# Modulation of a two-layer diffusion step: row sums on VectorE in place of matmuls, and inputs and outputs laid out ahead

## The chip, the cores and the metric

The kernel runs on one core of a Trainium2 chip. The metric is the time of one execution on the device in microseconds (us), the median of several runs.

## The reference

One inference step of a small trunk with two layers. 128 context tokens and 256 latent tokens, 384 in all, have 1024 features each, in float32. Each layer is a SwiGLU feed-forward block (hidden width 2816), a mixer (attention in layer 0, a gated spatial unit in layer 1), and a second feed-forward block. Ahead of each of these six blocks the activations are normalised and modulated, and after it a gate scales what is added:

```python
def modulation(cond, w, b):
    m = jax.nn.silu(cond) @ w + b                 # w is 1024 x 9216 for each layer
    return m.reshape(cond.shape[0], 1, N_MOD, D_MODEL)

def adaln_input(h, mod, j, g):
    return rms_norm(h, g) * (1 + mod[:, :, 3 * j + 1]) + mod[:, :, 3 * j]

hp = hp + 0.5 * adaln_gate(m_ctx, 0) * swiglu(adaln_input(hp, m_ctx, 0, norm_g[i, 0]), ffn1_w_gu[i], ffn1_w_down[i])
hs = hs + 0.5 * adaln_gate(m_lat, 0) * swiglu(adaln_input(hs, m_lat, 0, norm_g[i, 0]), ffn1_w_gu[i], ffn1_w_down[i])
```

So `modulation` is a product of two vectors (the conditions of context and of latent tokens) with two matrices of 1024 x 9216: 75 MB of weights, each used for two columns only. The rest is large matrix products with the 384 tokens.

## The kernel before

**Weights in panels.** All projections run through 169 panels of 1 MB, 256 columns (or 256 rows) of a weight matrix each. SyncE's queue loads a panel into `raw` (two buffers), ScalarE rounds it to `w_hi`, VectorE makes the remainder `w_lo = raw - w_hi` (`split`), and TensorE multiplies three times, hi by hi, hi by lo and lo by hi. Both parts have two buffers. A feed-forward block has 11 pairs of gate and up panels (`loop_pairs`, one `pair` each, called g = 0 to 10 here) and 11 down panels (`down`). The first pair of a block starts while its input x is still made, one piece of 128 features k after the other (`project_first` on TensorE, `make_x` on ScalarE and VectorE).

**Order.** Each engine runs its own instruction list in order and waits on semaphores at places written by hand. SyncE's queue issues nearly all transfers: panels p, p+1, and behind them a block of modulation weights (`mod_block`). The issue of panel p waits until VectorE has split panel p-2.

**Modulation.** The columns of the modulation matrices are cut into 72 blocks of 256. Blocks 0 to 7 (shift and scale of the first block) are needed at once. TensorE multiplies seven of them by the conditions as rows (`mod_rows`, L1037), ScalarE copies the rows to SBUF, and TensorE transposes them (L1045). The 64 blocks 8 to 71 are done beside the other work, in 30 pairs, in 8 down panels of each of three blocks, in 2 panels of the attention output, and in 4 panels each of the attention input (`MOD_STEPS`) and of the gated unit. For each, VectorE accumulates over k = 0 to 7 and both conditions into `macc` (`mod_sum`, 2 instructions at L751 and 14 at L754, of 256 elements), TensorE sums over partitions with a column of ones (`mod_psum`, 4 matmuls, shown as 8 instructions at L1055), and VectorE adds the bias (`mod_out`, L762). `mraw` holds two blocks, so the load of block b waits for the sums of block b-2:

```python
if b0 >= MOD_FIRST + 2:
    sp.wait_ge(macc_done, b0 + ii - MOD_SUM - 1)
```

**Beginning and end.** x and the small vectors arrive with tokens (or rows) on partitions and are transposed by TensorE (L1203, L1211). After the first pair's loads SyncE's queue issues small tables, and behind panels 2 and 3 the 32 loads of the attention bias (`load_bias`, L391), which GpSimd then masks (L495). At the end TensorE transposes each piece of h (L1390), ScalarE copies it to `y_tok` (L714), and eight transfers store it (L463, L464).

## Time and profile before

| | us |
|---|---|
| median of 3 runs | 1719.64 (1719.63 to 1720.17) |
| span of the profiled execution, first to last instruction | 1717.1 |
| TensorE busy with matmuls in it | 1660.1 |
| VectorE busy | 1067.5 |
| ScalarE busy | 578.3 |

The profile gives the profiled execution by its span; the median of the runs lies 2.5 us above it, for what comes before the first and after the last instruction. Busy times count an engine's own instructions; matmuls are pipelined, so TensorE's busy time is no measure of its peak.

### The profile page before, as it was taken

The page shows a single profiled execution, that of the slowest core. Times are in us where ns is not written, and L with a number is a line of the kernel's source. Part 1 is how long each engine was busy: PE and PEld are TensorE (multiplying, and loading weights), DVE is VectorE, ACT ScalarE, POOL GpSimd, SP SyncE. Part 2 cuts the span into 40 slices and gives each one's busy share as a digit, 9 for nine tenths or more (in the row PEclk, how much of TensorE's full clock was granted, in tenths as well). Part 3 has the DMA queues.
Part 4 walks back from the last instruction along what each step waited for, and adds up shares of the span by engine and source line. Part 5 has one row for each costly group of instructions (what it writes and reads, how often), then busy time and mean ns, then how long its engine had stood idle before and what let it go on. Part 6 is the DMA issues. An engine that isn't in the chain of part 4 may idle for free.

```text
span 1717.1 us, 25878 instructions
## 1 busy us (share of the span) xinstructions
PE 1660.1 (97%) x9927; PEld 1589.1 (93%) x9927; DVE 1067.5 (62%) x1803; ACT 578.3 (34%) x751; POOL 81.3 (5%) x48
## 2 busy tenths in 40 slices
PE   8899999988899899999989999998999998999998
PEld 4899999988756899999989999998999998999998
DVE  3677668767754766767966777697745435334323
ACT  2423232253344442322234333222642325333222
POOL 1200000034100100000010000001000001000000
PEclk9999999989999899999989999999999998999999
DMA  9755547526200445555634545564533332433332
GB/s 310 187 182 164 192 159 244 170 85 207 77 1 31 157 146 173 177 189 196 224 120 135 193 161 195 190 226 157 186 124 96 125 123 85 136 122 122 124 130 77
DMA packets 222917, 261.81 MB, mean 152 GB/s; under 512 B 14502, under 2 KB 207494, under 8 KB 222854
## 3 DMA queue, kind: packets, MB, share of 16 engines
q1 hardware_dynamic: 222854, 260.95, 46.3%
q8 instruction: 42, 0.69, 0.2%
q14 instruction: 21, 0.17, 0.0%
HBM read 258.64 MB, written 2.29 MB: 152 GB/s over the span
## 4 chain that ended last, share of the span: by engine, by line
PE 86%; issue 6%; DVE 4%; ACT 1%; POOL 1%; DMA 0%; POOLq 0%; SPq 0%; ACTq 0%; DVEq 0%
PE ps L1066 15%; PE ps L1067 15%; PE ps L1069 15%; PE ps L1022 9%; PE ps L1024 9%; PE ps L1023 9%; PE ps L1055 3%; PE ps L1037 2%; PE ps L1257 1%; DVE macc L754 1%; PE ps L1126 1%; PE ps L1294 1%; POOL hrs L503 1%; PE ps L1363 1%; DVE w_lo L731 1%
## 5 line engine op out<-in xcount | busy, mean ns | idle before, releaser
L731 DVE TENSOR_TENSOR w_lo<-raw,w_hi 128x2048 fp32r<-128x2048 f32 x164 | 380.0, 2317 | 282.3 <-ACT w_hi L527 282.2
L1066 PE MATMUL ps<-x_hi,w_hi 128*128 128x384 f32 x1536 | 523.3, 341 | 13.2 <-ACT x_hi L553 9.9
L1067 PE MATMUL ps<-x_hi,w_lo 128*128 128x384 f32 x1536 | 520.1, 339 | 0.0
L1069 PE MATMUL ps<-x_lo,w_hi 128*128 128x384 f32 x1536 | 517.1, 338 | 0.0
L527 ACT ACTIVATE w_hi<-raw 128x2048 fp32r<-128x2048 f32 x169 | 322.9, 1911 | 344.2 <-PE ps L1024 326.3
L754 DVE SCALAR_TENSOR_TENSOR macc<-mraw,cT,macc 128x256 f32<-128x256 f32 x896 | 359.9, 478 | 0.0
L1066 PEld LDWEIGHTS ps<-x_hi,w_hi 128*128 128x128 f32 x1536 | 292.1, 190 | 17.0 <-issue 13.3
L1067 PEld LDWEIGHTS ps<-x_hi,w_lo 128*128 128x128 f32 x1536 | 292.1, 190 | 0.0
L1069 PEld LDWEIGHTS ps<-x_lo,w_hi 128*128 128x128 f32 x1536 | 291.3, 190 | 0.0
L1022 PE MATMUL ps<-act_hi,w_hi 128*128 (+1 forms) x832 | 281.8, 339 | 0.0
L1024 PE MATMUL ps<-act_hi,w_lo 128*128 (+1 forms) x832 | 279.6, 336 | 0.0
L1023 PE MATMUL ps<-act_lo,w_hi 128*128 (+1 forms) x832 | 279.5, 336 | 0.0
L1022 PEld LDWEIGHTS ps<-act_hi,w_hi 128*128 128x128 f32 x832 | 156.5, 188 | 0.0
L1023 PEld LDWEIGHTS ps<-act_lo,w_hi 128*128 128x128 f32 x832 | 156.5, 188 | 0.0
L1024 PEld LDWEIGHTS ps<-act_hi,w_lo 128*128 128x128 f32 x832 | 156.4, 188 | 0.0
L569 ACT ACTIVATE act_hi<-tmp 128x768 f32 (+1 forms) x44 | 37.2, 846 | 291.4 <-DVE tmp L830 291.4
L1079 PE MATMUL ps<-w_hi,x_hi 128*128 128x256 f32 x408 | 118.0, 289 | 10.7 <-DVE qk_g L916 4.9
L830 DVE TENSOR_TENSOR tmp<-ps,tmp 128x768 f32<-128x768 f32 x44 | 42.1, 957 | 128.8 <-PE ps L1069 128.8
L1080 PE MATMUL ps<-w_lo,x_hi 128*128 128x256 f32 x408 | 116.7, 286 | 0.0
L1082 PE MATMUL ps<-w_hi,x_lo 128*128 128x256 f32 x408 | 114.6, 286 | 0.0
L565 ACT ACTIVATE tmp<-ps 128x768 f32<-128x768 f32 x44 | 35.7, 812 | 205.5 <-PE ps L1069 205.4
L1079 PEld LDWEIGHTS ps<-w_hi,x_hi 128*128 128x128 f32 x408 | 80.3, 197 | 13.3 <-issue 7.0
(154 smaller groups left out, 1310.7 us busy)
## 6 DMA issues: line engine op xcount, KB each, us to landing
raw<-ffn_w_gu SPq DMA_DIRECT2D x88, 1024.0 KB, 5.1
mraw<-mod_w SPq DMA_DIRECT2D x66, 1024.0 KB, 7.4
raw<-ffn_w_down SPq DMA_DIRECT2D x44, 1024.0 KB, 4.8
raw<-sgu_w_in SPq DMA_DIRECT2D x16, 1024.0 KB, 5.5
raw<-attn_w_in SPq DMA_DIRECT2D x9, 1024.0 KB, 5.0
raw<-sgu_w_out SPq DMA_DIRECT2D x8, 1024.0 KB, 4.8
mfirst<-mod_w SPq DMA_DIRECT2D x6, 1024.0 KB, 12.8
raw<-attn_w_out SPq DMA_DIRECT2D x4, 1024.0 KB, 4.9
```

What stands on the lines that cost most here:

```text
L527: nc.scalar.activation(w_hi[q0 % 2][:, :], raw[q0 % 2][:, :], ACT.Copy).then_inc(hi_done, 1)
L731: nc.vector.tensor_tensor(w_lo[q0 % 2][:, :], raw[q0 % 2][:, :], w_hi[q0 % 2][:, :].bitcast(F32), ALU.subtract).then_inc(lo_done, 1)
L754: last = nc.vector.scalar_tensor_tensor(acc, w, cc, acc, ALU.mult, ALU.add)
L1022: mm(out, w[0][:, cols], xs[0], start=start, stop=False)
L1023: mm(out, w[0][:, cols], xs[1], start=False, stop=False)
L1024: return mm(out, w[1][:, cols], xs[0], start=False, stop=stop)
L1066: mm(out, hi[:, cols], x_hi[:, k, :], start=(k == 0), stop=False)
L1067: mm(out, lo[:, cols], x_hi[:, k, :], start=False, stop=False)
L1069: last = mm(out, hi[:, cols], x_lo[:, k, :], start=False, stop=(k == KD - 1))
L1079: mm(out, x_hi[:, k, tok], hi[:, cols], start=(k == 0), stop=False)
L1080: mm(out, x_hi[:, k, tok], lo[:, cols], start=False, stop=False)
L1082: last = mm(out, x_lo[:, k, tok], hi[:, cols], start=False, stop=(k == KD - 1))
```

## The change

The host now hands over arrays that are laid out already: x with features on partitions, each panel as 128 rows of 8 KB, the modulation matrices transposed (`mod_rows`: 144 tiles of 128 outputs x 1024 inputs), the spatial matrix transposed, the small vectors as columns, and y is taken with features on partitions.

A block is now two tiles with outputs on partitions. For each tile and condition, one VectorE instruction multiplies 1024 elements by the condition, which is spread over all partitions in `cB`, and sums along the row. `mod_psum` is gone from TensorE. `mraw` holds one block, each tile with its own semaphore. For the first block, the shift's 8 tiles are made so on VectorE, one in each step of `make_x`, and the scale's 8 tiles with 8 small matmuls each on TensorE. The transposes at beginning and end are gone.

```diff
-        mraw = [sb(f"mraw{i}", [P, KD, MB]) for i in range(2)]
+        mraw = [sb(f"mraw{i}", [P, D]) for i in range(MT)]
...
+            def cond_sums(tile, ii, rows, out):
+                for cond in range(2):
+                    if tile or cond:
+                        dve.wait_ge(mchain, 2 * tile + cond + 2 * MT * ii)
+                    nc.vector.scalar_tensor_tensor(mprod[:, :], rows, 1.0, cB[:, cond, :], ALU.mult, ALU.mult,
+                                                   accum_out=out[:, cond:cond + 1]).then_inc(mchain, 1)
...
             def mod_sum(b0, ii):
...
-                            last = nc.vector.scalar_tensor_tensor(acc, w, cc, acc, ALU.mult, ALU.add)
+                n = b0 - MOD_FIRST
+                dve.wait_ge(mod_done, n + 1 + ii)
+                for a in range(MT):
+                    dve.wait_ge(mraw_in[a], 16 * (n + 1) + 16 * ii)
+                    cond_sums(KD + MT * n + a, ii, mraw[a][:, :], msc[:, a, :])
...
             def mod_block(b0, ii):
-                if b0 >= MOD_FIRST + 2:
-                    sp.wait_ge(macc_done, b0 + ii - MOD_SUM - 1)
+                for a in range(MT):
+                    if b0 > MOD_FIRST or not isinstance(ii, int):
+                        sp.wait_ge(mchain, 2 * KD + 2 * MT * (b0 - MOD_FIRST - 1) + 2 * a + 2 + 2 * MT * ii)
+                    sp.dma_start(mraw[a][:, :], mod_rows[bass.ds(MT * (b0 + ii) + a, 1), :, :].rearrange("a p k -> p (a k)")) \
                        .then_inc(mraw_in[a], 16)
...
+            sp.dma_start(cT[:, :, :], cond_cols).then_inc(c_in, 16)
+            sp.dma_start(cB[:, :, :], cond_rows.rearrange("(o c) k -> o c k", o=1).to_broadcast([P, 2, D])).then_inc(cb_in, 16)
+            sp.dma_start(vec[:, :], vecs).then_inc(vec_in, 16)
             sp.dma_start(ident[:, :], consts[0]).then_inc(const_in, 16)
+            sp.dma_start(h[:, :, :], x_in_t).then_inc(x_in, 16)
+            for k in range(KD):
+                sp.dma_start(mscale[:, k, :], mod_scale[k]).then_inc(mscale_in[k], 16)
+                sp.dma_start(mshift[:, k, :], mod_rows[k]).then_inc(mshift_in[k], 16)
+                if k < 2:
+                    panel(k, 0)
...
+            def first_mod(k):
+                dve.wait_ge(mshift_in[k], 16)
+                cond_sums(k, 0, mshift[:, k, :], shsum[:, k, :])
+                dve.wait_ge(mchain, 2 * k + 2)
+                nc.vector.tensor_scalar(modT[:, k, :], shsum[:, k, :], mbT[:, k:k + 1], None, ALU.add)
+                dve.wait_ge(mod_pe, k + 1)
+                nc.vector.tensor_scalar(aT[:, k, :], ps[:, 6 + k % 2, 0:2], mb1[:, k:k + 1], ngT[:, k:k + 1], ALU.add, ALU.mult) \
+                    .then_inc(mvec, 1)
...
+            def mod_scale_tile(k):
...
+                for kk in range(KD):
+                    last = mm(ps[:, 6 + k % 2, 0:2], mscale[:, k, P * kk:P * kk + P], cT[:, kk, :],
+                              start=(kk == 0), stop=(kk == KD - 1))
...
             for i in range(KD // 2):
-                sp.wait_ge(y_done, 2 * i + 2)
+                sp.wait_ge(h_done, KD * 5 + 2 * i + 2)
+                sp.dma_start(y_t[:, m:m + 2, :], h[:, m:m + 2, :]).then_inc(stored, 16)
```

In `make_x` of the first block `first_mod(0)` and `first_mod(k + 1)` come ahead of the VectorE half of piece k, and TensorE's `mod_scale_tile(k + 1)` ahead of its matmuls of piece k (k = 1 to 6). `mod_out` now follows `mod_sum` on VectorE at once, except in a pair, where it follows the product.

## Rows read from the trace of the kernel before

**Rows 1.** Page, the chain that ended last: shares of the span by engine.

```profile
PE 86%; issue 6%; DVE 4%; ACT 1%; POOL 1%; DMA 0%; POOLq 0%; SPq 0%; ACTq 0%; DVEq 0%
```

**Rows 2.** Timeline, ScalarE's silu: start, length, instruction; two blocks' pairs 1 and 10.

```profile
926.87 0.81 ACT L565 ACTIVATE tmp<-ps 128x768 f32<-128x768 f32 x1 [4.75 <-PE ps L1069]
...
1084.59 0.81 ACT L565 ACTIVATE tmp<-ps 128x768 f32<-128x768 f32 x1 [5.38 <-PE ps L1069]
...
1459.09 0.81 ACT L565 ACTIVATE tmp<-ps 128x768 f32<-128x768 f32 x1 [4.75 <-PE ps L1069]
...
1608.77 0.81 ACT L565 ACTIVATE tmp<-ps 128x768 f32<-128x768 f32 x1 [4.48 <-PE ps L1069]
```

**Rows 3.** Timeline, down panels with a modulation block (TensorE), and without (ScalarE).

```profile
307.95 0.95 PE L1055 MATMUL ps<-ones,macc 128*128 128x1 f32 x8
...
317.16 0.95 PE L1055 MATMUL ps<-ones,macc 128*128 128x1 f32 x8
...
1675.33 1.92 ACT L527 ACTIVATE w_hi<-raw 128x2048 fp32r<-128x2048 f32 x1 [6.40 <-PE ps L1024]
1683.65 1.92 ACT L527 ACTIVATE w_hi<-raw 128x2048 fp32r<-128x2048 f32 x1 [6.40 <-PE ps L1024]
```

**Rows 4.** Groups by line and shape: count, busy us, mean ns of one, idle before.

```profile
L731 DVE TENSOR_TENSOR w_lo<-raw,w_hi 128x2048 fp32r<-128x2048 f32 x164 | 380.0, 2317 | 282.3 <-ACT w_hi L527 282.2
L754 DVE SCALAR_TENSOR_TENSOR macc<-mraw,cT,macc 128x256 f32<-128x256 f32 x896 | 359.9, 478 | 0.0
...
L632 ACT ACTIVATION_READ_ACCUMULATOR prob<-ps,nmax 128x1 f32 x48 | 9.6, 200 | 0.0
```

**Rows 5.** Timeline, VectorE in a down panel: the idle time before its split.

```profile
315.15 2.29 DVE L731 TENSOR_TENSOR w_lo<-raw,w_hi 128x2048 fp32r<-128x2048 f32 x1 [0.85 <-ACT w_hi L527]
...
317.88 5.63 DVE L754 SCALAR_TENSOR_TENSOR macc<-mraw,cT,macc 128x256 f32<-128x256 f32 x14
```

**Rows 6.** Windows: length, busy us of each engine, clock, DMA share, GB/s.

```profile
0.00:51.10 51.10, 41.40 (x195) 20.11 (x196) 17.14 (x37) 12.86 (x20) 4.46 (x11) 0.93 0.98 314
```

**Rows 7.** Timeline of the beginning, several engines.

```profile
18.91 0.52 ACT L539 ACTIVATE sq<-h 128x384 f32<-128x384 f32 x1 [14.97 <-DVE h L869]
...
28.93 0.16 DVE L791 TENSOR_SCALAR ms<-ps 128x3 f32<-128x3 f32 x1 [6.80 <-PE ps L1126]
...
51.10 0.66 PE L1066 MATMUL ps<-x_hi,w_hi 128*128 128x384 f32 x1 [2.75 <-ACT x_hi L553]
...
69.30 0.96 DVE L830 TENSOR_TENSOR tmp<-ps,tmp 128x768 f32<-128x768 f32 x1 [0.88 <-PE ps L1069]
...
72.98 6.75 DVE L731 TENSOR_TENSOR w_lo<-raw,w_hi 128x2048 fp32r<-128x2048 f32 x1 [0.85 <-ACT w_hi L527]
...
92.38 0.45 PE L1066 MATMUL ps<-x_hi,w_hi 128*128 128x384 f32 x1 [1.15 <-DVE w_lo L731]
```

**Rows 8.** Timeline of the attention input's last panels: SyncE's queue, ScalarE, VectorE.

```profile
425.31 0.37 SPq L345 DMA_DIRECT2D raw<-attn_w_out  x1
...
439.82 1.93 ACT L527 ACTIVATE w_hi<-raw 128x2048 fp32r<-128x2048 f32 x1
...
437.93 5.62 DVE L754 SCALAR_TENSOR_TENSOR macc<-mraw,cT,macc 128x256 f32<-128x256 f32 x14
443.47 2.28 DVE L731 TENSOR_TENSOR w_lo<-raw,w_hi 128x2048 fp32r<-128x2048 f32 x1
...
457.13 0.17 DVE L762 TENSOR_TENSOR modT<-ps,mbT 128x16 f32<-128x16 f32 x1
```

**Rows 9.** Page, transfers: count, size, us from issue to landing.

```profile
raw<-attn_w_out SPq DMA_DIRECT2D x4, 1024.0 KB, 4.9
```

**Rows 10.** Timeline of the end: last update of h, transposes, last store's issue.

```profile
1708.61 0.74 DVE L851 SCALAR_TENSOR_TENSOR h<-ps,gT,h 128x128 f32<-128x128 f32 x2 [0.30 <-PE ps L1024]
...
1708.72 2.81 PE L1390 MATMUL ps<-ident,h 128*128 128x128 f32 x24
...
1713.89 0.45 SPq L464 DMA_DIRECT2D out<-y_tok  x1
```

More of the change, by code:

```diff
@@ L800, in rms, with make_x @@
                     half(1).then_inc(lo_done, 1)
-            def make_x(n):
+            def make_x(n, beside=lambda k: None):
                 dve.wait_ge(rb_done, n + 1)
@@ L845, in step @@
                         mod_sum(block + j0, 2 * i)
+                        mod_out(block + j0, 2 * i)
                 steps_beside_blocks(dve, 0, blocks, n - 2, step)
@@ L980, in _ @@
                     mod_sum(MOD_V + g, 0)
+                    mod_out(MOD_V + g, 0)
             dve.wait_ge(vss_done, 8)
@@ L1097, in project_first @@
                 for k in range(shared):
+                    beside(k)
                     if k == 0:
@@ L1146, in pair, with down, panel @@
                     project(feature_major, q + 2 * g0 + 1, ii, 2)
-                    if b is not None:
-                        pe.wait_ge(mod_done, outs_until(b - 1) + ii)
-                        mod_psum(b, ii, 6 + b % 2, 0, True)
                 loop_pairs(f, pe, pair)
-            def down(q0, n, idx, hi, lo, ready, block=0, blocks=0):
-                def panel(j0, i, beside=False, first=False, final=False):
+            def down(q0, n, idx, hi, lo, ready):
+                def panel(j0, i, first=False, final=False):
                     pe.wait_ge(lo_done, q0 + j0 + 2 * i + 1)
@@ L1167, in panel @@
                             last.then_inc(out_done, 1)
-                        if k == 3 and beside:
-                            mod_psum(block + j0 - 2, 2 * i, ORDER[-1], SPARE + 4 * (j0 - 2) + 8 * i, False)
                     if not final:
@@ L1178, in down @@
                 panel(1, 0)
-                steps_beside_blocks(pe, 2, min(blocks, n - 3), n - 1, panel)
-                panel(n - 1, 0, beside=blocks == n - 2, final=True)
+                steps_beside_blocks(pe, 2, 0, n - 1, lambda j0, i, beside: panel(j0, i))
+                panel(n - 1, 0, final=True)
             def ready_ffn(f):
@@ L1236, in _ @@
                 project(token_major, Q_IN0 + g, 0, QBANK[g % 2])
-                for b in range(MOD_IN - 1):
-                    if MOD_PSUM[b] == g:
-                        mod_psum(MOD_M + b, 0, 4, 4 * b, True)
             pe.wait_ge(gained, 4)
@@ L1386, in _ @@
             down(Q_F[3] + 2 * GU, GU, 5, act_hi, act_lo, ready_ffn(3))
-            for k, m in enumerate(ORDER):
-                pe.wait_ge(h_done, KD * 6 + k + 1)
-                for t in range(TT):
-                    last = nc.tensor.transpose(ps[:, m, P * t:P * t + P], h[:, m, P * t:P * t + P], ident[:, :])
-                last.then_inc(yT_pe, 1)
 PAIRS = (0, GU, 2 * GU, 3 * GU + 8)
@@ new lines, in columns, with rows, weight_panels, ffn @@
+def columns(w, order):
+    k, n = w.shape
+    p = w.reshape(k // P, P, n // 256, 256).transpose(2, 1, 0, 3)
+    return p[list(order)].reshape(len(order), P, PW)
+def rows(w):
+    k, n = w.shape
+    return w.reshape(k // 256, 2, P, n).transpose(0, 2, 1, 3).reshape(k // 256, P, PW)
+def weight_panels(i):
+    def ffn(gu, down):
+        half = GU
+        return [columns(gu, [g + half * up for g in range(GU) for up in range(2)]), rows(down)]
+    out = []
+    for layer in range(DEPTH):
+        out += ffn(i["ffn1_w_gu"][layer], i["ffn1_w_down"][layer])
+        if layer == 0:
+            out += [columns(i["attn_w_in"][0], QKV_ORDER), rows(i["attn_w_out"][0])]
+        else:
+            out += [columns(i["sgu_w_in"][0], [8 + g for g in range(8)] + list(range(8))), rows(i["sgu_w_out"][0])]
+        out += ffn(i["ffn2_w_gu"][layer], i["ffn2_w_down"][layer])
+    return np.concatenate(out)
@@ L1452 @@
     r = run(nc, [arrays], core_ids=[0])
-    return tuple(r.results[0][f"out_{i}"] for i in range(len(_OUTS)))
+    out = [r.results[0][f"out_{i}"] for i in range(len(_OUTS))]
+    y = out[0].transpose(2, 1, 0).reshape(T, D)
+    return (np.ascontiguousarray(y[CTX])[None], np.ascontiguousarray(y[LAT])[None], *out[1:])
```

350 lines of the change are left out of this document (108 added, 242 removed).

## Prediction

> **What bounds the kernel now.** I read the page first, then the chain of waits, then the timeline of each stage. TensorE does 86% of the chain [rows 1], so in most of the kernel a microsecond taken from TensorE's list is a microsecond of time, and work on VectorE counts only where TensorE waits for it. The timeline shows both sorts of place. A feed-forward block's pairs with a modulation block in each take (1084.59 - 926.87) / 9 = 17.52 us, those of the last feed-forward block, which has none, (1608.77 - 1459.09) / 9 = 16.63 us [rows 2]; ScalarE's silu waits for TensorE in all of them. A down panel with a block takes 9.21 us, one without 8.32 us [rows 3]. So the sums over partitions at L1055 cost TensorE 0.89 us for each block. The other places are the beginning (TensorE starts the first pair at 51.10 and stands again until 92.38 [rows 7]) and the attention input, where VectorE works without a gap from the sums through a split to the rotation of q and k, and TensorE waits for it until 457.13 [rows 8].
>
> **The steady part.** Of the 64 blocks beside other work, block 8 lies in the beginning and four in the attention input. The other 59 stand where TensorE is the bound: 59 x 0.89 = 52.5 us come off, if VectorE keeps up.
>
> Does it? The new instruction isn't in the trace. The nearest rows: L754, the same instruction with two float32 operands in SBUF, takes 0.478 us for 256 elements, and the subtraction at L731 2.317 us for 2048 [rows 4]. That is 1.03 ns for each further element, so 1024 elements take 0.478 + 768 x 0.00103 = 1.27 us. The sum output is the unknown. Below: nothing, the sum comes with the last element. Above: a separate read of the accumulator, as ScalarE has it at L632, 0.20 us [rows 4]. I take 1.31 us, near the lower end, each waiting for the one before. A block is then 4 x 1.31 = 5.2 us (6.0 with the upper price) and about 0.2 for the bias, against 6.2 us now (from the end of the split at 317.44 to 323.51, [rows 5]). In a down panel VectorE needs 2.29 + 5.4 = 7.7 of 8.32 us; it keeps up to 1.45 us for one instruction. In a pair it has more room.
>
> A rule speaks against this. The Trainium skill (Vector Engine (DVE) Microarchitecture Reference, section 7) says that this instruction with two SBUF sources that aren't bf16 runs at half throughput, having no port left for the accumulator. L754 shows full rate with such sources, but without a sum output [rows 4], so the trace contradicts the rule as written and leaves its reason open. By the rule the sum would be a loss; it is the first rival below.
>
> **The single buffer for blocks.** `mod_block` of block b now waits for the sums of b-1, and SyncE's queue holds the next panel behind it. In a pair this costs nothing: the next panel waits for the split that follows these sums anyway. In the down panels it is new: panel p+4 is issued after the sums that follow the split of p+2, not after that split. The loop is issue of two tiles and panel about 0.9, landing 4.9 [rows 9] and about 1 for the tile ahead of it, rounding 1.92 [rows 3], split 2.29 [rows 5], sums and bias 5.4: 16.4 us for two panels, against 2 x 8.32 = 16.64. It just fits, and a panel's halves are ready some 4 us before TensorE wants them (8.32 - 1.92 - 2.29), so a small drift over eight panels is absorbed. I cost it at nothing there; at 2 us more of landing it would cost 1 us a panel, less 4 us for each of three blocks, 12 us in all.
>
> **The attention input is where it bites.** The load of its fourth block waits for the sums of its third, which end at 437.93 + 5.62 = 443.55. The first panel of the attention output stands behind it in the queue: now issued at 425.31 and rounded at 439.82 [rows 8]. Afterwards it can be issued only when those sums are done. VectorE's chain there gets 0.8 us shorter for each of three blocks, so that is some 442. Landing takes 5 to 6 us more, rounding 1.9: VectorE, which has the split next at 443.47, gets it at about 450, 6 us late or more. It then splits (2.3), does the fourth block (5.4) and rotates (457.13 - 451.8, where the fourth block's sums end by my count, 5.3): 463, against 457.1. TensorE has finished its panels by then and waits, as do the scores. About 1.2 us come back, since the transposes that waited for `mod_out` no longer do. Net a loss of 4.5 us instead of a gain of 4 x 0.89 = 3.6. Bounds: 8 lost, 4 gained. The attention output has the same pattern, with four stores in the queue ahead of the next block's first panel: I take 2 us lost, bounds 0 and 3.
>
> **The beginning.** Ahead of the first piece of x now come the conditions spread over partitions (1.05 MB), the vectors and x (1.57 MB). At 314 GB/s [rows 6] x is there at about 11.5 us, not 18.9. The norm took 28.93 - 18.91 = 10.0 us [rows 7], then 1.7 for the power and the diagonal, then VectorE has two splits of 2.3: it can start `make_x` near 28. But each step now holds two sums (2.6), two small instructions (0.35) and the two of before (0.96): 3.9 us, 8 steps and the first two products 31 us. That ends at 59; two or three steps wait some 0.5 for the scale's matmuls; then x_hi 1.5, x_lo 0.6, and 36 matmuls of 0.173 = 6.2 that can't start before the last piece: 68, against 69.30 [rows 7]. So the earlier start is spent on the slower ramp. The loads don't decide it: all 13.3 MB are in by 13.3 / 0.314 = 42 us. What follows stays: SyncE's queue loads the bias in the same place, and GpSimd's masking holds VectorE's split at 72.98 to 6.75 us [rows 7] (2.29 alone), a collision that I expect again with at most a shift. The sums after it are 0.8 shorter. I take panel 4's start at 88, against 92.38: 4.4 us gained. Bounds: 84.3 if nothing collides (67.7 + 16.6), 98 if the ramp runs badly.
>
> **End and transposes.** h is finished at 1708.61 + 0.74 = 1709.35, and the last store is issued at 1713.89, 3.2 us before the end of the span [rows 10]. Now the store can be issued at 1709.4, so 4.5 us are gained (3 to 5). The eight transposes of the spatial matrix go: a third of the 24 at L1390, 0.9 us.
>
> **Sum.** 52.5 + 4.4 - 4.5 - 2 + 4.5 + 0.9 = 55.8 us. The profiled span of 1717.1 becomes 1661.3, and the median, 2.5 us above the span, 1719.64 - 55.8 = **1663.8 us**.
>
> **Rivals.**
> - *The sum output halves the rate* (2.35 us an instruction). For it: no row has this instruction with a sum. Against: full rate at L754. A block costs 9.6 us. The ramp gets 16 x 1.04 = 17 longer; a pair's chain on VectorE (sums, split, product, remainder, split: 18.1 us) passes 16.63, 0.6 worse than now over 29 pairs, 17; a down panel takes 11.9 against 9.21, 24 x 2.7 less 12 of slack, 53; the attention input 18, the gated unit 4; less 5 at the end. 104 slower: 1824 us. It turns to a loss at about 1.9 us an instruction. Chance 0.07.
> - *The queue's wait drags in the down panels and after* (tiles and panel land later than now): 12 to 24 us lost, 1676 to 1688 us. For it: the margin is 0.2 us in 16.6. Chance 0.12.
> - *The ramp stalls.* TensorE's granted clock is at half after a pause (0.66 us for the first matmul at 51.10, 0.34 at full [rows 7]). If it stays there in the ramp, a step's 12 matmuls and the scale tile take 7 us, and VectorE waits for the tile up to 3.8 us: about 15 more, 1679 us. Against: TensorE is busy in most of each step. Chance 0.1.
> - *The attention input costs nothing* (the panel lands in time for the rotation, or the gain there is had): 1655 us. Chance 0.13.
> - *It doesn't do what it says* (L1055's time comes back as another wait on TensorE): within 0.2%, about 3.4 us, which is what a measurement can tell from no change here. Chance 0.01.
>
> The forecast has 0.57. It and the three near rivals give faster 0.92; same 0.01; slower 0.07. The range takes the best of all bounds, 52.5 + 8.1 + 4 + 5 + 0.9 = 70.5 (1649), and the ramp or the queue badly: 1649 to 1688.
>
> **What would show it.** Pairs at 16.6 and blocks' down panels at 8.3 to 8.4 us; the sum instruction at 1.2 to 1.5 us; SyncE's attention output panel issued at 440 less what is gained by then, with VectorE idle before its split for 5 us or more; the first pair ending at 66 to 70; the end 3.3 us after the last h. A sum instruction above 1.5 us, or down panels above 8.5, would make the prediction wrong.

## The result, and the profile after

The changed kernel takes 1692.44 us (1691.21 to 1697.67, 4 runs), the kernel before 1719.91 us beside it (4 runs): ratio 0.984, 95% interval 0.983 to 0.986. So 27.5 us are gained where 55.8 were forecast, and the time lies 4 us above the range. The profiled execution took 1691.21 us, with a span of 1689.4 us.

The table takes the two traces apart between the same events, in us gained: the third pair's silu, the norms' mean squares on VectorE (`ms`), the first maximum of the scores, the last output piece of the attention (`x_hi`), and the end of the last update of h. The forecast's column is the prediction's own terms, its 59 blocks put where they stand.

| stretch | forecast | measured | off |
|---|---|---|---|
| start to the third pair's silu | +4.4 | -10.8 | -15.2 |
| rest of the first feed-forward block | +15.1 | +10.7 | -4.4 |
| attention input | -4.5 | -5.7 | -1.2 |
| attention itself | 0 | -6.4 | -6.4 |
| attention output | -0.2 | +2.1 | +2.3 |
| second feed-forward block | +16.0 | +17.5 | +1.5 |
| third feed-forward block | +16.0 | +13.5 | -2.5 |
| gated unit | +4.5 | +3.9 | -0.6 |
| fourth feed-forward block | 0 | -2.2 | -2.2 |
| end | +4.5 | +5.1 | +0.6 |

Two places hold most of it: the beginning, and the attention. What moves the time elsewhere is small and has both signs.

**The shares.** The chain that ended last, by engine; VectorE has 6% instead of 4 [rows 1], and there is a share for transfers.

```profile
PE 86%; DVE 6%; DMA 3%; issue 2%; ACT 2%; POOL 1%; SPq 0%; POOLq 0%; DVEq 0%; ACTq 0%
```

**The new instruction.** Groups by line and shape, as [rows 4]: count, busy us, mean ns of one, idle before.

```profile
L659 DVE SCALAR_TENSOR_TENSOR mprod<-mraw,cB 128x1024 f32<-128x1024 f32 x256 | 316.9, 1238 | 7.4
L659 DVE DVE_READ_ACCUMULATOR mprod<-mraw,cB 128x1 f32 x256 | 20.9, 82 | 0.0
...
L788 DVE TENSOR_SCALAR aT<-ps,mb,vec 128x2 f32<-128x2 f32 x8 | 2.2, 276 | 12.1 <-PE ps L950 12.1
```

A sum takes 1.24 us and a read of its accumulator 0.08, one every 1.27 us. The forecast had 1.31. The rule of the Trainium skill (Vector Engine (DVE) Microarchitecture Reference, section 7) that this form runs at half throughput is contradicted, now with a sum output: half the rate would be 2.35 us. The last line is new and belongs to the beginning: VectorE waits 12.1 us for the scale's matmuls.

**Pairs.** Timeline of ScalarE's silu, as [rows 2]: third block's pairs 1 and 10, then the fourth block's. A pair takes (1070.36 - 919.53) / 9 = 16.76 us, and (1585.36 - 1434.53) / 9 = 16.76 without blocks too.

```profile
919.53 0.81 ACT L501 ACTIVATE tmp<-ps 128x768 f32<-128x768 f32 x1 [4.82 <-PE ps L964]
...
1070.36 0.81 ACT L501 ACTIVATE tmp<-ps 128x768 f32<-128x768 f32 x1 [4.54 <-PE ps L964]
...
1434.53 0.82 ACT L501 ACTIVATE tmp<-ps 128x768 f32<-128x768 f32 x1 [4.82 <-PE ps L964]
...
1585.36 0.81 ACT L501 ACTIVATE tmp<-ps 128x768 f32<-128x768 f32 x1 [4.54 <-PE ps L964]
```

**The beginning.** Timeline of several engines, against [rows 7]. TensorE starts at 31.94 instead of 51.10. At 48.20 a tile of the scale takes 3.41 us, and VectorE's L788 waits for it; at 35.92 a tile of the same size took 1.92. From 48.20 to 67.20 a tile starts every 6.3 us, and this is the loop: the tile (3.41), the wait for VectorE's L788 and x_lo, which stand behind it (0.84), and six matmuls of the piece (2.08); VectorE's own 3.8 us of work fit into it. Then GpSimd masks the attention bias from 66.17 on, for 10.28 us, and a sum beside it takes 5.41 and a two-element instruction 4.33 us. The last piece of x comes at 78.27, and the first pair's copy (ScalarE's `act_hi`, which ends a pair) at 87.36, against 70.29 before.

```profile
31.94 0.66 PE L961 MATMUL ps<-x_hi,w_hi 128*128 128x384 f32 x1 [1.59 <-ACT x_hi L489]
...
35.92 1.92 PE L950 MATMUL ps<-cT,mscale 128*128 128x2 f32 x16
...
48.20 3.41 PE L950 MATMUL ps<-cT,mscale 128*128 128x2 f32 x16
...
51.64 0.28 DVE L788 TENSOR_SCALAR aT<-ps,mb,vec 128x2 f32<-128x2 f32 x1 [3.42 <-PE ps L950]
...
52.44 0.69 PE L961 MATMUL ps<-x_hi,w_hi 128*128 128x384 f32 x1 [0.84 <-DVE x_lo L729]
...
54.52 3.41 PE L950 MATMUL ps<-cT,mscale 128*128 128x2 f32 x16
...
66.17 10.28 POOL L427 TENSOR_TENSOR bias<-bias,maskT 128x2048 f32<-128x2048 f32 x2 [44.73 <-DMA bias<-toep_scratch]
...
66.69 5.41 DVE L659 SCALAR_TENSOR_TENSOR mprod<-mshift,cB 128x1024 f32<-128x1024 f32 x1
...
72.15 4.33 DVE L786 TENSOR_SCALAR modT<-shsum,vec 128x2 f32<-128x2 f32 x1
...
87.36 0.85 ACT L505 ACTIVATE act_hi<-tmp 128x768 fp32r<-128x768 f32 x1 [3.60 <-DVE tmp L744]
```

The same copy in the kernel before:

```profile
70.29 0.84 ACT L569 ACTIVATE act_hi<-tmp 128x768 fp32r<-128x768 f32 x1 [3.50 <-DVE tmp L830]
```

**The attention input.** Timeline of SyncE's queue, ScalarE and VectorE, against [rows 8]. The panel stands behind the block's load until the sums are done, is issued at 441.04 and rounded at 447.90; VectorE has stood for 9.00 us. The last rotation ends at 461.69 + 0.82 = 462.5; the forecast was 463.

```profile
441.04 11.45 SPq L292 DMA_DIRECT2D raw<-panels  x3
...
447.90 1.91 ACT L459 ACTIVATE w_hi<-raw 128x2048 fp32r<-128x2048 f32 x1 [9.04 <-DMA raw<-panels]
...
449.84 2.29 DVE L651 TENSOR_TENSOR w_lo<-raw,w_hi 128x2048 fp32r<-128x2048 f32 x1 [9.00 <-ACT w_hi L459]
...
461.69 0.82 DVE L814 TENSOR_TENSOR qk_g<-qk_g,tmp 128x640 f32<-128x640 f32 x1
```

**The clock.** Windows: length, busy us of PE, PEld, DVE, ACT and POOL, granted clock, DMA share, GB/s. From 48 to 78 us the granted clock is 0.50, that is 1.2 GHz. After the attention input, where TensorE waits 5.2, 2.0, 0.7 and 0.6 us, it is at 0.56 to 0.61 for 30 us, the lower level in most of them; before, it was 1.00 from 465 us on.

```profile
32.00:48.00 16.00, 14.32 (x68) 14.15 (x69) 11.98 (x27) 4.54 (x9) 0.00 (x0) 0.84 1.06 362
48.00:66.00 18.00, 15.49 (x65) 15.23 (x64) 9.54 (x21) 4.36 (x9) 0.00 (x0) 0.50 0.64 106
66.00:78.00 12.00, 5.42 (x24) 5.33 (x23) 11.06 (x7) 1.43 (x4) 10.28 (x2) 0.50 0.01 1
...
455.00:465.00 10.00, 7.93 (x27) 5.20 (x26) 9.18 (x20) 2.14 (x8) 0.00 (x0) 0.61 0.41 155
465.00:475.00 10.00, 8.73 (x24) 4.82 (x25) 2.88 (x9) 4.43 (x13) 0.00 (x0) 0.56 0.00 0
475.00:485.00 10.00, 10.00 (x28) 5.39 (x27) 2.74 (x9) 2.73 (x9) 0.00 (x0) 0.59 0.01 2
```

A window of the kernel before:

```profile
465.00:475.00 10.00, 10.00 (x43) 5.61 (x41) 5.47 (x18) 5.10 (x18) 0.00 (x0) 1.00 0.00 0
```

**The end.** The last update of h starts at 1685.97 and takes 0.74 us, so 2.7 us are left to the end of the span, against 1717.1 - 1709.35 = 7.7 [rows 10].

```profile
1685.97 0.74 DVE L766 SCALAR_TENSOR_TENSOR h<-ps,gT,h 128x128 f32<-128x128 f32 x2 [0.30 <-PE ps L937]
```

### The profile page after: what moved, and what is told of

It is laid out like the page before. It is cut to its first block, busy times and chain, and to the rows that moved or that the text cites. A ratio compares the mean times of both kernels' runs of the same rounds, so it can differ in the third digit from the quotient of the medians.

```text
span 1689.4 us, 23807 instructions
## 1 busy us (share of the span) xinstructions
PE 1616.0 (96%) x9348; PEld 1559.3 (92%) x9348; DVE 1005.7 (60%) x1338; ACT 575.3 (34%) x738; POOL 84.5 (5%) x48
## 4 chain that ended last, share of the span: by engine, by line
PE 86%; DVE 6%; DMA 3%; issue 2%; ACT 2%; POOL 1%; SPq 0%; POOLq 0%; DVEq 0%; ACTq 0%
PE ps L961 16%; PE ps L962 16%; PE ps L964 16%; PE ps L935 8%; PE ps L936 7%; PE ps L937 7%; DVE mprod L659 3%; DMA raw<-panels 2%; PE ps L974 2%; PE ps L977 2%; PE ps L975 2%; PE ps L1118 2%; PE ps L1023 1%; PE ps L1153 1%; ACT w_hi L459 1%
## 5 line engine op out<-in xcount | busy, mean ns | idle before, releaser
L651 DVE TENSOR_TENSOR w_lo<-raw,w_hi 128x2048 fp32r<-128x2048 f32 x164 | 375.7, 2292 | 294.6 <-ACT w_hi L459 293.8
L961 PE MATMUL ps<-x_hi,w_hi 128*128 128x384 f32 x1536 | 523.9, 341 | 19.5 <-DVE x_lo L729 10.8
L659 DVE SCALAR_TENSOR_TENSOR mprod<-mraw,cB 128x1024 f32<-128x1024 f32 x256 | 316.9, 1238 | 7.4
L961 PEld LDWEIGHTS ps<-x_hi,w_hi 128*128 128x128 f32 x1536 | 292.4, 190 | 23.4 <-issue 12.1
L744 DVE TENSOR_TENSOR tmp<-ps,tmp 128x768 f32<-128x768 f32 x44 | 42.1, 958 | 143.5 <-PE ps L964 143.5
```

Of the source, the lines that this page charges most:

```text
L651: nc.vector.tensor_tensor(w_lo[q0 % 2][:, :], raw[q0 % 2][:, :], w_hi[q0 % 2][:, :].bitcast(F32), ALU.subtract).then_inc(lo_done, 1)
L659: nc.vector.scalar_tensor_tensor(mprod[:, :], rows, 1.0, cB[:, cond, :], ALU.mult, ALU.mult, accum_out=out[:, cond:cond + 1]).then_inc(mch ...
L961: mm(out, hi[:, cols], x_hi[:, k, :], start=(k == 0), stop=False)
```

## The experiments

All are edits of the changed kernel. Times are medians of 4 runs, to be held against 1692.44; the stretches come from one profile each. Four runs of one of these kernels spread over 4 to 21 us, those of the kernel before over 3 to 6, so small differences are read in the traces.

### 1. The masks later

```diff
             for qt in range(2):
+                pool.wait_ge(silu_done, 3 + 2 * qt)
                 bv = bias[:, qt, :, :]
```

> The changed kernel, with GpSimd's two maskings of the attention bias held back until the gated unit of the first feed-forward has finished its third and its fifth activation; all work is kept. Theory A (collision in the ramp): in the changed kernel a row sum that starts at 66.69 us and a small multiply at 72.15 take 5.41 and 4.33 us instead of 1.22 and about 0.3 while GpSimd masks, in the stretch where VectorE sets the start of the first panel. Held back, both fall to their usual length, the first activation comes about 8 us earlier (75 instead of 82.97) and so does everything up to the tenth pair (about 239.5 instead of 247.5 us for its activation); the end comes 6 to 8 us earlier, about 1685. Theory B (TensorE sets the ramp): the stretched instructions lie beside a TensorE that is late anyway, the first activation moves by less than 2 us, and the time stays within 2 us of 1692. Theory C: the maskings stretch VectorE in the pairs in the same way, where it has no time to spare, and the 8 us come back there by the tenth pair.

Measured: 1690.02 us (ratio to before 0.982, 0.981 to 0.984). The first pair's copy comes at 81.94 instead of 87.36. The collision hasn't gone, it has moved into the pairs: the timeline of VectorE shows a sum of 5.53 us there.

```profile
107.78 5.53 DVE L660 SCALAR_TENSOR_TENSOR mprod<-mraw,cB 128x1024 f32<-128x1024 f32 x1
```

From copy to copy the pairs 2 to 5 take 17.43, 17.51, 17.43 and 17.31 us and those after them 16.77: 2.6 us come back, 1.5 of them as waits of TensorE for w_lo. So theory A holds, with 5.4 us instead of 8 (without the collision VectorE does what it did in the other steps and waits 2.45 us for the scale's tile), and theory C in part. The Trainium skill (SBUF — State Buffer, section Terms) has VectorE and GpSimd share a pair of ports that one holds for its full instruction; 1.2 us that become 5.5 beside masks of 4.9 us each agree with that.

### 2. The scale's matmuls two tiles ahead

```diff
-                if k >= 2:
-                    pe.wait_ge(mvec, k - 1)
+                if k >= 3:
+                    pe.wait_ge(mvec, k - 2)
                 for kk in range(KD):
-                    last = mm(ps[:, 6 + k % 2, 0:2], mscale[:, k, P * kk:P * kk + P], cT[:, kk, :],
+                    last = mm(ps[:, (6, 7, 4)[k % 3], 0:2], mscale[:, k, P * kk:P * kk + P], cT[:, kk, :],
...
-                                      (lambda k: mod_scale_tile(k + 1) if 0 < k < KD - 1 else None) if f == 0 else lambda k: None)
+                                      (lambda k: mod_scale_tile(k + 2) if 0 < k < KD - 2 else None) if f == 0 else lambda k: None)
...
             mod_scale_tile(1)
+            mod_scale_tile(2)
```

> The changed kernel, with the matmuls of the first modulation's scale made two tiles ahead of VectorE instead of one, in three banks of PSUM instead of two; all work is kept. Theory A (the two engines wait for each other in turn): in the changed kernel VectorE waits 12.1 us in all for the scale's matmuls in the ramp, and its steps are 6.3 to 6.5 us apart; with a tile more ahead the wait falls under 3 us. TensorE's own work of a step is then the bound while its clock is at half: 3.41 us of scale matmuls and 6 to 12 matmuls of some 0.35 us, 5.5 us in all, against about 4.0 us of VectorE's work, so that steps come down to 4.5 to 5.5 us and the ramp ends 4 to 8 us earlier, time 1685 to 1688. Theory B (the half clock is what costs): the steps are bound by TensorE's work at 1.2 GHz however far ahead it is, the steps stay above 6 us, and the time within 2 us of 1692.

Measured: 1681.23 us (ratio 0.977, 0.976 to 0.979). The steps fall to 3.79 us, VectorE's own work, which the forecast had at 3.9. The timeline of VectorE shows two x_lo in a row, 3.79 us apart, with no wait between them; GpSimd's masks now meet the second pair's split and sum, where they were before the change.

```profile
48.20 0.55 DVE L729 TENSOR_TENSOR x_lo<-tmp,x_hi 128x384 fp32r<-128x384 f32 x1
...
51.99 0.55 DVE L729 TENSOR_TENSOR x_lo<-tmp,x_hi 128x384 fp32r<-128x384 f32 x1
...
68.66 5.76 DVE L651 TENSOR_TENSOR w_lo<-raw,w_hi 128x2048 fp32r<-128x2048 f32 x1 [0.85 <-ACT w_hi L459]
74.34 5.62 DVE L659 SCALAR_TENSOR_TENSOR mprod<-mraw,cB 128x1024 f32<-128x1024 f32 x1
```

The first pair's copy comes at 65.97, 21.4 us earlier, more than theory A had: it had counted with a clock at half, and the clock stayed up. By the third pair's silu 15.6 us of them are left (96.24 instead of 111.81), since the collision costs 22.80 - 16.96 = 5.8 us in the second pair, as it did before the change (23.31 - 17.53 = 5.8). That alone makes up the 15.2 us that the beginning missed: it starts the third pair 4.8 us earlier than the kernel before, where 4.4 were forecast. ScalarE's silu of pairs 1 and 2:

```profile
73.44 0.81 ACT L501 ACTIVATE tmp<-ps 128x768 f32<-128x768 f32 x1 [4.81 <-PE ps L964]
...
96.24 0.81 ACT L501 ACTIVATE tmp<-ps 128x768 f32<-128x768 f32 x1 [6.61 <-PE ps L964]
```

Windows, with the columns as above; 0.81 where there was 0.50:

```profile
48.00:66.00 18.00, 18.00 (x97) 17.66 (x96) 11.99 (x22) 7.17 (x12) 0.00 (x0) 0.81 0.64 103
```

### 3. The load of the fourth block behind the panel

```diff
                 step(0, 0, False)
+                between()
                 step(1, 0, False)
...
-            down(Q_OUT0, KD // 2, MOD_M + MOD_IN, MOD_OUT)
+            down(Q_OUT0, KD // 2, MOD_M + MOD_IN, MOD_OUT, lambda: mod_block(MOD_M + 3, 0))
...
-MOD_LOAD = (5, 6, 8, 8)
+MOD_LOAD = (5, 6, 8, 9)
```

> The changed kernel, with the load of the modulation tiles for the last block of the attention's input moved on SyncE's queue from before the attention output's first weight panel to behind it, and that block's sums so one place later; all work is kept. Theory A: the wait of SyncE for the sums before it is what makes the last input panels late, TensorE's gap of 5.21 us ahead of 453.11 us and three small ones of 3.3 us in all come from there, and the granted clock of 0.56 to 0.61 from 455 to 485 us follows from the gaps. Without them the first scores start about 5 us earlier (463 instead of 468.3), the clock stays near 1.00 as in the kernel before (0.83 in one window only), and the attention takes 80 instead of 87 us: 10 to 12 us less in all, about 1681. Theory B: the attention is longer for another reason (its own order of engines), then 3 to 5 us less. Theory C: the gap comes from ScalarE's copy of the values and stays: within 1 us of 1692.

Measured: 1682.71 us (ratio 0.979, 0.976 to 0.981). From the norm's sums over partitions to the first maximum of the scores it takes 102.6 us instead of 112.3 (106.6 before the change). So the wait in the queue cost not only the 5.7 us against before but also the gain that was due there. The longest wait of TensorE from 440 to 460 us; the 5.2 us are gone:

```profile
PE ps L1141 <- ACT kT_na L555: 2.1, 1, 2.1
```

But the attention itself, first maximum to last output piece, stays at 97.4 us (97.6 in the changed kernel, 91.2 before), and the clock still falls. So theory A's sum (10 to 12 us less) is nearly met, by other terms than its own: it had 5 us from the earlier scores and 7 from the clock, and the traces show 9.7 and none. The half of it that tied the clock to the long wait falls.

```profile
455.00:465.00 10.00, 9.31 (x23) 4.71 (x21) 3.11 (x12) 3.33 (x10) 0.00 (x0) 0.50 0.00 0
```

### 4. Idle matmuls in the attention's waits

This kernel only adds work: 36 and 40 matmuls whose results nobody reads.

```diff
+                    for _ in range(36):
+                        mm(ps[:, 4, 0:T], x_hi[:, 0, 0:P], x_hi[:, 1, :], start=True, stop=True)
                     pe.wait_ge(qkv_act, 3)
...
                 elif g == 8:
+                    pe.wait_ge(tr_act, 4)
+                    for _ in range(40):
+                        mm(ps[:, 7, 0:T], x_hi[:, 0, 0:P], x_hi[:, 1, :], start=True, stop=True)
                     pe.wait_ge(rope_done, 1)
```

> The changed kernel with idle matmuls added: 36 into an unused bank of PSUM ahead of the wait of 5.21 us in the attention's input and 40 ahead of the wait for the rotated queries; nothing is taken away. They fill waits of TensorE and are there to hold its granted clock. Theory A (the 7 us that the attention is longer are the clock's): the scores start no earlier than before (468, or up to 3 us later where a filler is longer than its wait), the granted clock is near 1.00 from 465 us on instead of 0.56 to 0.61, the attention takes 80 to 82 instead of 87.2 us, and the time falls by 3 to 7 us, to 1685 to 1689. Theory B (the attention is longer for its own order, the clock beside it): the clock rises and the attention stays at 86 to 87 us; the time is 1692 to 1695.

Measured: 1687.10 us (ratio 0.980, 0.977 to 0.984). The stretch to the first maximum is as long as without fillers (112.3 us), and the attention takes 90.6 us instead of 97.6. The clock is at 1.00:

```profile
465.00:475.00 10.00, 9.31 (x42) 5.29 (x39) 5.00 (x16) 5.12 (x17) 0.00 (x0) 1.00 0.00 0
```

More work in less time: the 7 us are the clock's.

### 5. and 6. The three edits together, and with a filler

Experiment 5 has the edits of 1 to 3; 6 adds 16 idle matmuls where experiment 4 has its 40.

> The changed kernel with the edits of the first three experiments together: GpSimd's masks held back, the scale's matmuls two tiles ahead, and the load of the attention input's fourth block moved behind the attention output's first panel; all work is kept. If the losses are separate, they add: the scale ahead gave 14.4 us of span and the load order 9.7 of its 12.3 in the attention's input. In the trace with the scale ahead the mask still lies on one row sum of 5.63 us and on the panels behind it (first to second pair 21.0 us instead of 16.7), so holding it back should give 4 more. Span 1689.4 - 14.4 - 9.7 - 4 = 1661, time 1661 to 1667 with the spread of some 4 us that the last runs show. If the losses hide each other (a later stage wants the same time), it stays above 1670.

> The kernel of the three edits together, and 16 idle matmuls ahead of the wait for the rotated q and k, which add work (some 2.8 us) and take none away. Clock theory of the attention: with the load order mended the granted clock still fell to half from 464 to 481 us in the trace's own time and the attention still took 97.4 us from the first maximum to the last output piece, against 90.6 with fillers; 16 matmuls in the place of the waits of 2.1 and 0.7 us keep the clock near 1.00 in the scores, and the attention is 5 to 7 us shorter than without them, for 0 to 1 us of delay: 1656 to 1661. Rival: the fall isn't due to these waits but to the small transposes themselves; then the clock falls as before and the time is 0 to 2 us above the kernel without fillers.

Measured: 1670.76 us (ratio 0.972, 0.970 to 0.973) and 1665.92 us (0.970, 0.966 to 0.974). Both medians lie above what was expected (1661 to 1667, 1656 to 1661), and that of 5 lies by 0.8 us where losses that hide each other were to show. The profiled execution of 5 (1665.18 us, the fastest of its four) says that the gains add, nearly: the first copy is 21.6 us earlier (21.4 in experiment 2), and the attention's input 8.5 shorter (9.7 in experiment 3). The four runs spread over 8 us in 5 and over 13 in 6, and what lengthens the others isn't shown. In 5 the first pair's copy comes at 65.72 and the second's at 82.56, 16.8 us later and not 21.0 as in experiment 2 (pairs 2 to 5 pay 2.8 of it back, as in experiment 1); the attention takes 97.6 us, in 6 it takes 90.2. Windows of 435 to 445 us, first of 5, then of 6:

```profile
435.00:445.00 10.00, 9.31 (x23) 4.71 (x21) 3.06 (x12) 3.33 (x10) 0.00 (x0) 0.50 0.00 0
```

```profile
435.00:445.00 10.00, 7.98 (x52) 6.75 (x51) 7.11 (x18) 5.13 (x14) 0.00 (x0) 1.00 0.14 51
```

The ramp, the same in both programs, went otherwise: in 6 the clock was 0.63 from 48 to 66 us (0.81 in 5), and the first copy came at 72.79.

### 7. Idle matmuls in the ramp

The changed kernel with four matmuls ahead of each wait for x_lo in the first pair; only added work.

```diff
+                    if n == 0:
+                        for _ in range(4):
+                            mm(ps[:, 4, 0:T], x_hi[:, 0, 0:P], x_hi[:, 0, :], start=True, stop=True)
                     pe.wait_ge(x_done, KD * n + k + 1)
```

> The changed kernel, with four idle matmuls of 384 columns added on TensorE ahead of each wait for a piece of x_lo in the first pair (eight waits), into a bank that is free there; nothing is taken away and the scale stays one tile ahead. Clock theory of the ramp: the ramp is slow because the clock is at half in most of 42 to 84 us; kept busy, TensorE stays at 1.00, the scale's tile takes 1.92 instead of 3.41 us, VectorE's steps come from 6.4 down to 4.5 to 5 us, and the first pair comes 8 to 12 us earlier. Order theory (one tile ahead is too little at any clock): already at the full clock of the first steps VectorE waited 1.20 and 2.57 us; the steps stay at 5.5 us or more, the clock rises or not, and less than 5 us are gained; if the clock stays at half, the fillers make the ramp up to 5 us longer.

Measured: 1682.52 us (ratio 0.981, 0.976 to 0.986; three of the four runs at 1677.5 to 1683.8). The clock is at 0.86 from 48 to 66 us and 0.92 to 78 instead of 0.50, and the first copy comes at 75.00, 12.4 us earlier, though the tile is still only one ahead. VectorE still waits 7.1 us for it. Both theories have a part: the order makes the wait, the wait lets the clock fall, and the clock makes the wait longer.

```profile
48.00:66.00 18.00, 17.91 (x110) 16.95 (x109) 14.14 (x32) 6.05 (x12) 0.00 (x0) 0.86 0.68 107
66.00:78.00 12.00, 11.77 (x63) 11.45 (x62) 6.30 (x3) 5.27 (x4) 10.66 (x2) 0.92 0.26 88
```

### 8. The sums' matmuls given back

```diff
                     project(feature_major, q + 2 * g0, ii, 0)
+                    if f < 3:
+                        for _ in range(4):
+                            mm(ps[:, 4, 0:1], ident[:, :], ones[:, 0:1], start=True, stop=True)
...
+                    if beside:
+                        for _ in range(4):
+                            mm(ps[:, 7, T:T + 1], ident[:, :], ones[:, 0:1], start=False, stop=True, skip_group_check=True)
```

> The changed kernel, with the matmuls over partitions given back to TensorE without their use: four matmuls of one column (float32) for each modulation block that stands beside other work, 33 in the pairs and 24 in the down panels, 57 in all. It measures the main term of the prediction by itself. Prediction's theory (what left TensorE's list is what left the time): 57 x 0.89 = 51 us slower than the changed kernel, about 1743, pairs 0.9 us and down panels 0.9 us longer. Rival (the gain of 0.89 for each block was partly a wait for the sums that came and went with them): 0.3 to 0.6 us for each, 20 to 35 us slower.

The expectation miscounts: there are 30 blocks in the pairs and 24 in the down panels, 54 and not 57, as the groups show (8 instructions each), so that the theory's figure is 54 x 0.89 = 48 us.

```profile
L1045 PE MATMUL ps<-ones,ident 128*128 128x1 f32 x240 | 28.4, 239 | 0.0
L1079 PE MATMUL ps<-ones,ident 128*128 128x1 f32 x192 | 22.8, 240 | 0.0
```

Measured: 1739.72 us, slower than before the change (ratio 1.011, 1.008 to 1.013), and 47.3 us above the changed kernel's first median, 42.1 above its second (next experiment): 0.78 to 0.88 us a block. The span is 50.0 us longer, 0.93 a block. The main term of the prediction holds; the rival falls.

### 9. The changed kernel once more

> The changed kernel once more, unchanged. In the nine traces so far a pair of panels in a steady stretch lasts 16.640, 16.768 or 16.960 us, with TensorE never idle and its granted clock at 1.00, and the level holds for a pair and the down panels of one feed-forward block and changes from block to block. Theory A (a matter of the execution, not of the program): the levels in this trace stand otherwise than in the first one of the same program (16.960, 16.640, 16.768, 16.769 in the four feed-forward blocks), and the end differs by 1 to 6 us from that alone. Theory B (of the program: where its instructions lie): the same four levels again, to 0.01 us. The clock's stretches at half in the ramp and in the attention should be there again, and the median near 1692.

Measured: 1697.65 us (1690.81 to 1702.27; ratio 0.988, 0.985 to 0.991). Theory A holds. Timeline of the silu, pairs 1 and 10 of the second and of the third block, in this execution:

```profile
628.31 0.81 ACT L501 ACTIVATE tmp<-ps 128x768 f32<-128x768 f32 x1 [4.91 <-PE ps L964]
...
780.87 0.81 ACT L501 ACTIVATE tmp<-ps 128x768 f32<-128x768 f32 x1 [4.64 <-PE ps L964]
...
921.42 0.81 ACT L501 ACTIVATE tmp<-ps 128x768 f32<-128x768 f32 x1 [4.75 <-PE ps L964]
...
1071.10 0.81 ACT L501 ACTIVATE tmp<-ps 128x768 f32<-128x768 f32 x1 [4.48 <-PE ps L964]
```

That is 16.95 and 16.63 us a pair, where the first execution had (782.02 - 632.33) / 9 = 16.63 and 16.76, of the same program, without blocks' work on TensorE in either and with the clock at 1.00.

### 10. A longer block

```diff
+                for a in range(2):
+                    if n + a or not isinstance(ii, int):
+                        dve.wait_ge(mspare, 2 * n + a + 2 * ii)
+                    nc.vector.tensor_tensor(spare[:, :], cB[:, 0, 0:512], cB[:, 1, 0:512], ALU.mult).then_inc(mspare, 1)
```

> The changed kernel with two more products of 128x512 elements on VectorE at the end of each modulation block, whose result nobody reads: about 1.5 us more for a block, 5.5 to 7.0. It measures how near VectorE and the single buffer are to being the bound. By the prediction's count a down panel's VectorE work of 7.7 us becomes 9.2, over the 8.32 us of TensorE, and SyncE's loop for two panels (16.4 of 16.64 us) 19.4: VectorE alone would make the down panels with a block 0.9 us longer, less 4 us of slack for each feed-forward block, some 10 us in all; the loop 1.4 us each, 20 us; and 5 us more in the attention's input. 1702 to 1718. The pairs, with over 3 us of room, stay as they are. Rival: the loads land sooner than counted, the margin is wider, the down panels don't lengthen, and only the attention's input pays: 1695 to 1698.

Measured: 1700.62 us (ratio 0.989, 0.987 to 0.991). The span is 7.1 us longer, of which 4.9 lie in the attention's input. The three blocks' down panels stay within 2 us of what they took (93.1, 93.1 and 93.4 us for eight with a block and what follows, against 93.5, 91.8 and 93.0). VectorE's timeline in a down panel, split to split 8.96 us:

```profile
1112.49 2.29 DVE L653 TENSOR_TENSOR w_lo<-raw,w_hi 128x2048 fp32r<-128x2048 f32 x1
...
1120.11 1.42 DVE L682 TENSOR_TENSOR spare<-cB 128x512 f32<-128x512 f32 x2
1121.45 2.28 DVE L653 TENSOR_TENSOR w_lo<-raw,w_hi 128x2048 fp32r<-128x2048 f32 x1
```

VectorE has no idle time there, so its own work is the bound, 0.6 us a panel over TensorE's 8.32, and the slack takes up most of it: at one pitch of the matmuls the stretches are 0.7 to 1.6 us longer. The median lies between the theory's figures and the rival's; the trace, where the attention's input pays and the down panels hardly do, goes with the rival, but its reason isn't shown. The expectation counts the longer block twice in the queue's loop; once gives 16.4 + 1.4 = 17.8 us for two panels, which VectorE's own 2 x 8.96 = 17.9 covers. So this kernel doesn't refute that the loop just fits in 16.64; it shows that a block of 6.7 us is still nearly free.

### 11. The three edits with both fillers

As experiment 6, and in the scale's tiles 3 to 7:

```diff
                     pe.wait_ge(mvec, k - 2)
+                    for _ in range(2):
+                        mm(ps[:, (6, 7, 4)[k % 3], 0:T], x_hi[:, 0, 0:P], x_hi[:, 0, :], start=True, stop=True)
```

> The three edits and the attention's filler together, with two idle matmuls of 384 columns more ahead of each of the scale's tiles 3 to 7 in the ramp (0.35 us each tile at the full clock). With the scale ahead the ramp's length still depended on how long the clock was at half near its end: 7 us at half in one trace (first pair's copy at 68.9 us) and 14 in another (76.0). Theory: TensorE's wide matmuls among the scale's narrow ones keep the clock up, the ramp ends at 66 to 70 us, and the time is 1658 to 1662 with less spread. Rival: TensorE is the bound of these steps, the fillers only make them longer, and the time stays at 1664 to 1670.

(The 68.9 and 76.0 of this text are 65.72 and 72.79 in the traces' own time.)

Measured: **1661.98 us** (1660.03 to 1664.94; ratio 0.967, 0.964 to 0.969), the fastest of the edited kernels. The first copy comes at 72.49: in this trace the fillers didn't bring the ramp to the 65.7 of experiment 5, though its clock was 1.00 to 48 us and 0.84 to 66. The attention takes 90.2 us. Pairs 2 to 5 are at 17.2 to 17.4 again. So the time is in the theory's range, but not by the ramp that it had.

### 12. The masks in the last down panels

```diff
-                pool.wait_ge(silu_done, 3 + 2 * qt)
+                pool.wait_ge(pe_done, Q_F[0] + 2 * GU + 8 + qt)
```

> The kernel with the three edits and both fillers, with GpSimd's two masks held back further, to the first feed-forward block's last down panels, which have no modulation block beside them. In the traces with the masks in the pairs, pairs 2 to 5 took 17.2 to 17.5 us instead of 16.8, and TensorE waited 1.5 us for w_lo there: the masks weren't free in the pairs, as the first reading of the first experiment had it, but cost 2.6 us. Theory A (they cost where VectorE has a block beside the pair's own work): a down panel without a block needs 2.3 us of VectorE's time in 8.3, a split that takes 6 to 7 us beside the mask still comes in time, pairs 2 to 5 fall to the length of the others, nothing is longer at the masks' new place, and the time is 1658 to 1660 against 1662. Theory B (pairs 2 to 5 are long for another reason, they were so with the scale ahead too): they stay at 17.2 to 17.5 us, and the time is within 1 us of 1662, or up to 3 us above it if the last panels suffer.

Measured: 1673.77 us (1663.80 to 1681.52, 6 runs; ratio 0.972, 0.969 to 0.975), 12 slower than experiment 11 and above both theories' figures, more than the down panels account for. Pairs 2 to 5 are as long as the others, so the first half of theory A holds: the masks cost 2.6 us there. The second half falls. The down panels' stretch is 98.9 us instead of 92.5. VectorE makes the split two panels ahead of TensorE and the blocks with it, so while TensorE is in panel 8 VectorE is still at the last two blocks, and both masks meet a sum; the timeline of VectorE and TensorE:

```profile
309.51 5.52 DVE L661 SCALAR_TENSOR_TENSOR mprod<-mraw,cB 128x1024 f32<-128x1024 f32 x1
...
318.88 5.60 DVE L661 SCALAR_TENSOR_TENSOR mprod<-mraw,cB 128x1024 f32<-128x1024 f32 x1
...
319.12 0.44 PE L937 MATMUL ps<-act_hi,w_hi 128*128 x1 [1.90 <-DVE w_lo L653]
...
331.02 0.44 PE L937 MATMUL ps<-act_hi,w_hi 128*128 128x384 f32 x1 [1.71 <-DVE w_lo L653]
```

And in this trace the clock fell in the attention though the 16 idle matmuls were there (0.54 and 0.50 from 445 to 465 us), and the attention took 98.7 us. So 16 of them hold the clock in some executions and not in others; experiment 11's four runs had it each time by their mean clock (0.978 to 0.980), this kernel's six in some (0.972 to 0.979). Experiment 11's median may owe something to that.

## Why the prediction was wrong, step by step

- **The step that failed is the beginning**, "two or three steps wait some 0.5 for the scale's matmuls", and from it 68 us for the first pair and +4.4. All other numbers of that step were good: with the tile two ahead the steps are 3.79 us (3.9), the first pair's product starts at 64.98 (68), and 4.8 us are gained at the third pair (4.4). But TensorE works at the tile (1.92 us) and the x matmuls (12 of them in a step at the start, six from the fourth on, 0.17 to 0.32 each) in turn with VectorE's L788 and x_lo (0.84), one tile ahead. The prediction added up VectorE's work of a step (3.9) and never this loop: by these rows some 4.8 us with 12 matmuls even at the full clock, and 6.3 with six once the clock has fallen to 1.2 GHz and the tile takes 3.41. VectorE waited 12.1 us in five waits, not 1 to 1.5. The rival "the ramp stalls" had this very mechanism and its 15 us, and got 0.1. Experiments 2 and 7 show both halves.
- **The collision with GpSimd** was expected "again with at most a shift", and that was right: it shifted from the second pair into the ramp and costs 5.4 us there (experiment 1) where it cost 5.8 (experiment 2), so it has no part in the 15.2 us. In later pairs it costs 2.6 to 2.8 (experiments 1 and 5), in the down panels some 5.4 (experiment 12, 98.9 against 93.5 at its pitch): the same 10 us of GpSimd's work in four places.
- **The attention itself** had no term. A loss in its input was forecast to 0.5 us (463), but not that the waits let the clock fall for the next 30 us: 6.4 us (experiments 4 and 6). The row that could have warned is the same as in the ramp, a first matmul of 0.66 us after a pause [rows 7]; the 0.34 us that the prediction sets beside it stands in the trace but not in those rows.
- **The attention input** was right in mechanism, and 1.2 us short in size.
- **The steady part** (52.5 us) was right in mechanism, and 0.78 to 0.93 us a block is what it measured at. It came out smaller in this execution by the pitch of the matmuls, the time from the start of one to the start of the next (below): in the first block a pair took (247.49 - 111.81) / 8 = 16.96 us, in the third and fourth 16.76, where 16.63 was forecast, and that is nearly all of the -4.4, -2.5 and -2.2 in the table. The one trace of the kernel before stood at the short pitch in all its feed-forward blocks (17.53 us less 0.89, and 16.64), and the forecast took it for the only one.
- **VectorE keeping up and the end** (5.1 us for 4.5) were right; the 0.9 us of the gated unit's transposes aren't measured apart. That TensorE "stands again until 92.38" overstates [rows 7]: in the trace before, it waits twice for w_lo there, 3.3 us in all. The attention output, forecast at 2 us lost, lost nothing.
- **The queue's wait in the down panels** was counted as just fitting, and no loss shows there. A block of 6.7 us still nearly fits (experiment 10).

With the beginning and the attention mended the time is 1662.0 us, next to the 1663.8 that was forecast for a kernel without these losses; the two aren't the same sum, since the mended order also gains in the attention input and the ramp.

What stays open: why the clock falls in the ramp and in the attention in some executions and not in others with the same program for that stretch, and what sets the pitch.

## What to carry to other kernels

Where an engine's next input comes from an engine that waits for it, add up the loop through both and not the work of one, with TensorE at its lower clock, and give it a buffer more than the sum at full clock asks for. After a stretch of TensorE waits price what follows at the lower clock too, not only the wait; a few idle matmuls in a wait can be worth their time. When a stage is moved, look at what GpSimd does beside its new place: the same two masks cost 2.6 us in one place and 5.8 in another.

## What the runs showed of the hardware

- TensorE's pitch in a steady stretch isn't one number. With the clock at 1.00 and no idle time a pair of 96 matmuls took 16.64, 16.77 or 16.96 us wherever nothing else held TensorE, in fourteen traces, or 173.3, 174.7 and 176.7 ns from one 384-column matmul to the next. A feed-forward block's pairs and down panels share a level mostly, and it changes between blocks, where the clock has fallen and risen again, and between executions of one program (experiment 9). It moves the time by up to 2% of a block. That the rise of the clock sets it is a guess.
- A row sum with a sum output over 1024 float32 elements takes 1.22 us, and 0.08 for the accumulator.
- Beside one of GpSimd's sums of 128x2048 elements (4.9 us) even an instruction of two elements on VectorE took 4.33 us.
- In the changed kernel the granted clock was 0.56 to 0.61 for 30 us after TensorE's waits ahead of the scores. With 76 idle matmuls in these waits it was 1.00 (experiment 4); with 16 it was so in two traces (experiments 6 and 11) and not in a third (experiment 12).
